# Local attention placed between the chunks of the projection that feeds it

## What is computed

```
z = h @ w_in
q, k, v = split_cols(z[..., :SWA_COLS], (SWA_Q_COLS, SWA_KV_COLS, SWA_KV_COLS))
o_a = swa_sink_attention(q, k, v, sinks, alibi_slopes(SWA_HEADS))
o_b = rwkv7_time_mix(z[..., SWA_COLS:], mu, w0, w2, a0, a2, g2, k_k, k_a, r_k, ln_g, ln_b)
o = jnp.concatenate([o_a, o_b], axis=-1).astype(h.dtype)
return o @ w_out
```

```
s = jnp.einsum('bnqgrd,bnkgd->bngrqk', qb, kb)
s = s - slopes * dist                    # -inf outside the window
m = jnp.maximum(jnp.max(s, axis=-1, keepdims=True), sink)
p = jnp.exp(s - m)
p = p / (jnp.sum(p, axis=-1, keepdims=True) + jnp.exp(sink - m))
o = jnp.einsum('bngrqk,bnkgd->bnqgrd', p, vb)
```

## Time and profile before

| | |
|---|---|
| time, median of 3 runs | 2430.26 us (2426.51 to 2432.41) |
| profiled execution, its own time | 2425.49 us |
| its span (first to last instruction) | 2423.7 us |
| PE busy | 2128.3 us, 88% |
| DVE busy | 1620.8 us, 67% |
| ACT busy | 992.0 us, 41% |
| mean granted TensorE clock | 0.91 |

### The profile page before, as it was taken

One profiled execution on the slowest core, in us unless ns is written; L12 is line 12 of the kernel. 1 busy time (PEld: TensorE's weight loads), 2 busy tenths in 40 slices (PEclk: granted clock), 3 DMA queues, 4 the chain that ended last, 5 costly groups with the idle time before them and its releaser, 6 DMA issues.

```text
span 2423.7 us, 35322 instructions
## 1 busy us (share of the span) xinstructions
PE 2128.3 (88%) x14424; PEld 1908.3 (79%) x14424; DVE 1620.8 (67%) x2579; ACT 992.0 (41%) x1572; POOL 0.2 (0%) x4
## 2 busy tenths in 40 slices
PE   7729679999888899999999878489999999768998
PEld 7619569999865699999999855369999999456998
DVE  4467479884155698878857879658787753276555
ACT  4321054454144554443345633244334332345332
POOL 0000000000000000000000000000000000000000
PEclk9769589999877899999989999789998998878999
DMA  7200038746220487667644310047766652303551
GB/s 295 93 0 1 1 136 298 279 140 226 94 98 1 152 286 275 234 234 276 254 148 158 139 53 1 0 165 262 282 225 245 237 183 90 132 1 108 199 188 70
DMA packets 114849, 379.33 MB, mean 157 GB/s; under 512 B 4993, under 2 KB 5121, under 8 KB 113921
## 3 DMA queue, kind: packets, MB, share of 16 engines
q1 hardware_dynamic: 114688, 377.08, 43.3%
HBM read 376.01 MB, written 1.05 MB: 156 GB/s over the span
## 4 chain that ended last, share of the span: by engine, by line
PE 72%; DVE 20%; ACT 4%; issue 3%; DMA 2%; DVEq 0%; SPq 0%; ACTq 0%
PE psum L873 29%; PE psum L889 14%; PE psum L651 7%; PE psum L704 4%; DVE htok L1854 2%; DVE buf L569 2%; PE psum L645 2%; PE psum L1130 2%; PE psum L1483 1%; PE psum L2272 1%; DMA ring<-in_w_ffn 1%; PE psum L1727 1%; PE psum L856 1%; DVE buf L2053 1%; PE psum L498 1%
## 5 line engine op out<-in xcount | busy, mean ns | idle before, releaser
L873 PEld LDWEIGHTS psum<-buf,buf 128*128 128x128 f32 x6048 | 741.5, 192 | 12.9 <-DVE buf L787 4.0
L873 PE MATMUL psum<-buf,buf 128*128 128x256 f32 x6048 | 746.2, 283 | 2.0 <-DVE buf L787 2.0
L889 PE MATMUL psum<-buf,buf 128*128 128x512 f32 x1584 | 384.1, 391 | 3.3 <-DVE buf L936 3.3
L889 PEld LDWEIGHTS psum<-buf,buf 128*128 128x128 f32 x1584 | 289.1, 188 | 59.7 <-DVE buf L936 5.0
L787 DVE TENSOR_TENSOR buf<-ring,buf 128x2048 fp32r<-128x2048 f32 x132 | 301.9, 2287 | 43.3 <-ACT buf L781 42.4
L651 PE MATMUL psum<-buf,buf 128*128 128x256 f32 x2064 | 255.0, 284 | 9.5 <-DVE buf L569 9.4
L651 PEld LDWEIGHTS psum<-buf,buf 128*128 128x128 f32 x2064 | 249.2, 192 | 15.0 <-DVE buf L569 15.0
L781 ACT ACTIVATE buf<-ring 128x2048 fp32r<-128x2048 f32 x132 | 251.3, 1904 | 20.3 <-DMA ring<-in_w_ffn 20.3
L803 DVE TENSOR_TENSOR buf<-ring,buf 128x1024 fp32r<-128x1024 f32 x132 | 161.5, 1223 | 144.4 <-ACT buf L798 144.1
L569 DVE TENSOR_TENSOR buf<-ring,buf 128x1024 fp32r<-128x1024 f32 x132 | 161.3, 1224 | 118.0 <-ACT buf L563 108.7
L798 ACT ACTIVATE buf<-ring 128x1024 fp32r<-128x1024 f32 x132 | 139.3, 1055 | 191.6 <-PE psum L889 189.1
(11 more groups left out here) (318 smaller groups left out, 2362.0 us busy)
## 6 DMA issues: line engine op xcount, KB each, us to landing
ring<-in_w_ffn SPq DMA_DIRECT2D x88, 1536.0 KB, 6.5
modw<-in_w_mod SPq DMA_DIRECT2D x98, 768.0 KB, 6.9
ring<-in_w_conv SPq DMA_DIRECT2D x44, 1536.0 KB, 6.5
ring<-in_w_ssd_in SPq DMA_DIRECT2D x16, 1536.0 KB, 6.6
ring<-in_w_ns_in SPq DMA_DIRECT2D x9, 1536.0 KB, 7.6
ring<-in_w_hy_in SPq DMA_DIRECT2D x7, 1536.0 KB, 19.2
ring<-in_w_ssd_out SPq DMA_DIRECT2D x5, 1536.0 KB, 6.5
ring<-in_w_cmp SPq DMA_DIRECT2D x4, 1024.0 KB, 4.7
```

The source lines that it names most:

```text
L873: ins = E.matmul(b[:, g * T:(g + 1) * T], w[:, wa, g, k, :], h[:, ha, k, :], start=k + n_ == 0, stop=k == KC - 1 and n_ == 2)
L889: ins = E.matmul(acc[:, t, g * 512:(g + 1) * 512], hr[z][:, ha, t * P:(t + 1) * P], wd[z][:, wa, g * 512:(g + 1) * 512], start=j == 0 and ...
```

## The change

The attention is no longer run after the projection but between its chunks:

- The columns of `w_in` are laid out with the values behind the keys, so the value chunk is chunk 6, and the recurrent chunks are 7 to 20.
- `main` takes the list of PSUM banks for its chunks (`ring_of`) and a function `tick(c)` that it calls at the end of each chunk's turn. The first stage gives banks 6 and 7; the other projections keep the default of 4 to 7.
- `attend` is divided: `attention` makes the five steps (with `back` divided into `normalize` and `turn`), and takes places for its buffers, the number of pairs of score banks (`nsc`) and the first banks of transposes and outputs. Here scores use banks 0-1 only, transposes 2-3, outputs 4-5. `attend` calls them in the order as before for the other two stages that use it.
- `tick` gives unit `n` its steps at fixed chunks: scores and exponentials at chunk `7 + 3n`, normalize at `8 + 3n`, turn at `9 + 3n`, outputs and their copy at `10 + 3n`. The outputs of unit `n` stand ahead of the scores of unit `n + 1` at the same chunk. The last step is at chunk 19.
- The scores wait only for ScalarE up to the evacuation of chunk 6.
- `Ring.used` of a slot is now a list to which every chunk of the load adds its point.

```diff
@@ -170,7 +170,7 @@
     row("k_head_g", i["mla_k_head_g_2"][0])
 
     hy = i["hy_w_in"][0]
-    hy = np.concatenate([hy[:, 0:512], twice(hy[:, 512:640], 2), hy[:, 768:2560], hy[:, 640:768]], 1)
+    hy = np.concatenate([hy[:, 0:512], twice(hy[:, 512:640], 2), hy[:, 640:2560]], 1)
     ns = i["nsa_w_in"][0]
     kc, vc, ks, vs, kw, vw = (ns[:, 1024 + 256 * j:1280 + 256 * j] for j in range(6))
     ns = np.concatenate([ns[:, 0:1024], twice(kc, 4), twice(vc, 4), twice(ks, 4), twice(kw, 4), vs, vw,
@@ -584,6 +584,7 @@
                 if c % 3 == 0:
                     m = min(3, n - c)
                     made["slot"], made["full"] = load(dram[name][c:c + m], m)
+                    Ring.used[made["slot"]] = []
                 s, full = made["slot"], made["full"]
                 raw = slot_ap(s, SLOT)[:, (c % 3) * CHUNK:(c % 3 + 1) * CHUNK]
                 if c in tokens:
@@ -591,7 +592,7 @@
                 else:
                     p = split_chunk(raw, wp[c % 3], full, wp_free[c % 3])
                     made[c] = (s, raw, p)
-                    Ring.used[s] = [p]
+                    Ring.used[s].append(p)
 
             def pre_a(free):
                 wp_free[0] = wp_free[1] = free
@@ -602,7 +603,8 @@
                 wp_free[2] = free
                 prepare(2)
 
-            def main(evac, h_pts):
+            def main(evac, h_pts, ring_of=(4, 5, 6, 7), tick=None):
+                nb = len(ring_of)
                 freed = [()] * 3 + [(Ring.sums_taken,)]
                 done = []
                 first = 0
@@ -618,16 +620,16 @@
                             for c in range(2):
                                 w = wp[c].rearrange("p a (k n) -> p a k n", k=KC)
                                 for n_, (wa, ha) in enumerate(PASSES):
-                                    ins = E.matmul(bank(4 + c)[:, 0:T], w[:, wa, k, :], h[:, ha, k, :], start=k + n_ == 0,
+                                    ins = E.matmul(bank(ring_of[c])[:, 0:T], w[:, wa, k, :], h[:, ha, k, :], start=k + n_ == 0,
                                                    stop=k == KC - 1 and n_ == 2)
                                 if k == KC - 1:
                                     done.append(pe.count(ins.then_inc(pe.sem, 1)))
                     wp_free[0:2] = [done[0]], [done[1]]
-                    freed[0] = evac(0, bank(4), done[0])
+                    freed[0] = evac(0, bank(ring_of[0]), done[0])
                 for c in range(first, n):
                     prepare(c + 1)
                     s, raw, point_w = made[c]
-                    b = bank(4 + c % 4)
+                    b = bank(ring_of[c % nb])
 
                     @block.tensor
                     def _(_e):
@@ -635,7 +637,7 @@
                         if c == 0:
                             for point in h_pts:
                                 E.wait_ge(*point)
-                        for point in freed[c % 4]:
+                        for point in freed[c % nb]:
                             E.wait_ge(*point)
                         if c in tokens:
                             w = raw.rearrange("p (k n) -> p k n", k=KC)
@@ -652,12 +654,14 @@
                                                    stop=k == KC - 1 and n_ == 2)
                         done.append(pe.count(ins.then_inc(pe.sem, 1)))
                     if c in tokens:
-                        Ring.used[s] = Ring.used[s][-1:] + [done[c]] if c % 3 else [done[c]]
+                        Ring.used[s].append(done[c])
                     else:
                         wp_free[c % 3] = [done[c]]
                     if c:
-                        freed[(c - 1) % 4] = evac(c - 1, bank(4 + (c - 1) % 4), done[c - 1])
-                evac(n - 1, bank(4 + (n - 1) % 4), done[n - 1])
+                        freed[(c - 1) % nb] = evac(c - 1, bank(ring_of[(c - 1) % nb]), done[c - 1])
+                    if tick is not None:
+                        tick(c)
+                evac(n - 1, bank(ring_of[(n - 1) % nb]), done[n - 1])
 
             return pre_a, pre_b, main
 
@@ -1003,13 +1007,15 @@
             return dict(pre_a=pre_a, pre_b=pre_b, run=run, gain=gain, shift=shift, h=h)
 
 
-        def attend(units, keys, ready, at):
+        def attention(units, keys, ready, at, pt_at=None, st_at=None, nsc=2, turn_bank=4, out_bank=6):
             ar = Region(at)
             s_buf = [ar.take(4 * keys).rearrange("p (h k) -> p h k", h=4) for _ in range(3)]
 
+            ar.at = ar.at if pt_at is None else pt_at
             pT = [[[ar.take(4 * P) for _ in range(u_blocks)] for u_blocks in
                    [max(u["blocks"] for u in units if u["branch"] == b) for b in sorted({u["branch"] for u in units})]]
                   for _ in range(2)]
+            ar.at = ar.at if st_at is None else st_at
             st = ar.take(3 * 16)
             state = {"s_free": [go] * 2, "p_free": [go] * 3, "t_free": go, "o_free": [go] * 2,
                      "pT_free": [go] * 2}
...
@@ -1074,8 +1080,7 @@
                         p = act.count(A.activation(xtra, xtra, ACT.Exp).then_inc(act.sem, 1))
                     u["exp"] = p
 
-            def back(n, u):
-                q = n % 2
+            def normalize(n, u):
                 nk = u["keys"]
                 s = s_buf[n % 3]
                 stats = st[:, 16 * (n % 3):16 * (n % 3) + 16]
@@ -1091,16 +1096,20 @@
                         vl(V.tensor_tensor(rs, rs, u["gates"], ALU.mult).then_inc(dve.sem, 1))
                     Ring.p = vl(V.tensor_tensor(s[:, :, 0:nk], s[:, :, 0:nk],
                                                 spread(rs.rearrange("p (h o) -> p h o", o=1), [P, 4, nk]), ALU.mult).then_inc(dve.sem, 1))
-                normed = Ring.p
+                u["normed"] = Ring.p
+
+            def turn(n, u):
+                nk = u["keys"]
+                s = s_buf[n % 3]
 
                 @block.tensor
                 def _(_e):
-                    E.wait_ge(*normed)
+                    E.wait_ge(*u["normed"])
                     E.wait_ge(*state["t_free"])
                     for b in range(u["blocks"]):
                         w = min(P, nk - b * P)
                         for i in range(4):
-                            ins = E.transpose(bank(4 + b)[0:w, i * P:(i + 1) * P], s[:, i, b * P:b * P + w], ident)
+                            ins = E.transpose(bank(turn_bank + b)[0:w, i * P:(i + 1) * P], s[:, i, b * P:b * P + w], ident)
                     Ring.p = pe.count(ins.then_inc(pe.sem, 1))
                 state["p_free"][n % 3] = Ring.p
 
...
@@ -1143,6 +1152,10 @@
 
 
 
+            return scores, exponentials, normalize, turn, outputs, outputs_copy
+
+        def attend(units, keys, ready, at):
+            scores, exponentials, normalize, turn, outputs, outputs_copy = attention(units, keys, ready, at)
             scores(0, units[0])
             for n in range(len(units) + 3):
                 if n + 1 < len(units):
@@ -1152,7 +1165,8 @@
                 if 2 <= n < len(units) + 2 and units[n - 2]["last"]:
                     outputs(units[n - 2])
                 if 1 <= n <= len(units):
-                    back(n - 1, units[n - 1])
+                    normalize(n - 1, units[n - 1])
+                    turn(n - 1, units[n - 1])
                 if n >= 3 and units[n - 3]["last"]:
                     outputs_copy(units[n - 3])
             return [(dve.sem, dve.n), (act.sem, act.n), (pe.sem, pe.n)]
@@ -1160,7 +1174,7 @@
 
         def hybrid():
             h = halves(H_AT, KC)
-            pre_a, pre_b, project = projection("w_hy_in", 21, h, tokens=(20,))
+            pre_a, pre_b, project = projection("w_hy_in", 21, h, tokens=(6,))
 
             def run(h_pts, nxt):
                 return hybrid_run(h_pts, project, nxt)
@@ -1200,13 +1214,13 @@
                     def _(_e):
                         A.wait_ge(*p)
                         Ring.q = act.count(A.activation(kT[:, c - 4, :], b[:, 0:T], ACT.Copy).then_inc(act.sem, 1))
-                elif c == 20:
+                elif c == 6:
                     @block.scalar
                     def _(_e):
                         A.wait_ge(*p)
                         Ring.q = act.count(A.activation(vtok, b[:, 0:T].rearrange("p (t d) -> p t d", t=NT), ACT.Copy).then_inc(act.sem, 1))
                 else:
-                    m = c - 6
+                    m = c - 7
                     dst = ([r_] * 4 + [k_] * 4 + [v_] * 4)[m][:, (m % 4) * T:(m % 4 + 1) * T] if m < 12 else \
                         (wa if m == 12 else glo)
 
@@ -1225,8 +1239,6 @@
                                                                  dst[:, 1:T], ALU.mult, ALU.add).then_inc(dve.sem, 1))
                 return (Ring.q,)
 
-            project(evac, h_pts)
-            projected = [(dve.sem, dve.n), (act.sem, act.n), (pe.sem, pe.n)]
             oT = hT
 
 
@@ -1244,7 +1256,27 @@
                              out=oT[:, 2 * g:2 * g + 2, t * P:(t + 1) * P])
                     u["parts"] = [u]
```

(28 more changed lines are left out.)

## The result

| | before | changed |
|---|---|---|
| median | 2425.84 us (7 runs, 2425.22 to 2432.41) | 2443.6 us (7 runs, 2437.21 to 2445.94) |
| profiled execution | 2425.49 | 2437.36 |
| tanh that begins the recurrent half | 108.30 | 120.34 |

A forecast was written before the change was run, and what follows sets the result against it. Projection bound by PE (TensorE). Work 9.6, pauses 19.0, chunk 2 0.4, tail 1.0, less 26.2 removed: +3.8; clock +8.9, low-rank -0.5: +12.2 us on 2430.3, said as 2442, range 2430 to 2450.

The forecast's parts named there:

- Pauses, 19.0 us: Projection loop: PE stands still before chunks 9, 12, 15, 18, as splits queue behind the softmax: 4.0, 5.5, 4.0, 5.5 us.
- Work on TensorE, 9.6 us: Projection loop: attention matmuls between chunks count in full on PE: scores 3.2, outputs 3.5, transposes 2.9 us.
- Clock, 8.9 us: Projection loop: half clock for 3.0 to 6.0 us after each of four pauses, costing 2.2 us each.
- Low-rank matmuls, -0.5 us: Behind the attention: these matmuls may begin at full clock; between 0 and -4.7 us, -0.5 taken.
- Chunk 2, 0.4 us: Projection start: with two banks chunk 2 waits for the evacuation of chunk 0, about 0.4 us once.
- Tail, 1.0 us: After chunk 20: its evacuation, the wait of the tanh (L1258) and hand-overs, 1.0 us.
- Sum: Whole kernel: all terms give +12.2 us, so 2437.7 us for an execution like the profiled one.
- The median, 2442: Whole kernel: +12.2 us added to the median of three timed runs, 2430.3, gives 2442.5, said as 2442.
- Rival A: Projection loop: splits keep ahead, no stall or clock drop, only PE's own work added: 2414.5 us; chance 0.13.
- B: Projection loop: the stalls come but the clock stays full: +3.8 us, 2434; chance 0.15.
- C: Projection loop: half clock holds longer, up to 4.7 us lost per pause: +22.6, 2453; chance 0.08.

The follow-up runs named there:

- the run with the steps spread alone: Changed kernel with only each unit's attention steps spread over more chunks, softmax divided by engine, two banks, split still behind the tick: 2413.22 us, ratio 0.993.
- The loop without pauses: Changed kernel with weight split ahead of the softmax, three projection banks and attention steps spread over more chunks: 2412.14 us, ratio 0.9944.
- the run with extra matmuls: Changed kernel with 24 or 36 unused matmuls put on TensorE where it stood idle behind the chunk after each unit's scores: 2429.35 us, ratio 1.0016.
- the run without them: Changed kernel with unused extra matmuls in TensorE's pauses, loop at full clock: chunk 2 to tanh 85.7 us, 7.0 less than 92.7; median 2429.35 us.
- the spread versions: Changed kernel with attention steps spread: alone 2413.22 us; with split ahead, ratio 0.9947; with split ahead and three banks, 2412.14 us.
- the run with split ahead and three banks: Changed kernel with the weight split ahead of tick(c) and projection banks 5 to 7, softmax still in the tick of its scores: ratio 1.0009.

## Why the prediction was right, step by step

- *Pauses, 19.0 us.* Measured 17.8: 3.70 and 5.19 where 4.0 and 5.5 stood. From the end of chunk 7 (45.84 in the chain of waits) to the restart at 53.25 it is 7.4 us where 7.6 stood, since neighbouring instructions of one engine overlap by 0.1 us in the rows; and PE finished chunk 8 3.7 us behind chunk 7 where 3.6 stood. The mechanism was the one predicted, down to the evacuation that the second bank adds; the run with the steps spread alone removed it by order, with the same instructions.
- *Work on TensorE, 9.6 us.* The chain of waits gives 0.67 and 1.09 for the scores (the prediction had 0.87 for the wide ones), 0.44 and 0.87 for the transposes (so they do halve with the clock), 0.59 and 1.07 for the outputs: 9.5 in total. The loop without pauses says 10.5. The 1 us more, which I had not counted, lies where TensorE changes from one kind of matmul to another: in the run with extra matmuls a chunk behind scores took 2.98 us from its first matmul to the next group's, and one behind transposes 3.04, where 2.88 is a chunk among chunks.
- *Clock, 8.9 us.* The chunks behind the pauses took 4.60, 4.46, 4.61 and 5.46 us on the chain where others took 2.87, and one unit's transposes 1.24 for 0.87: 8.0 us, and 7.0 by the run without them. Half clock lasted 3.4, 3.4, 3.4 and 6.8 us; counted from the restart on, as the prediction counts, it is 3.4, 3.0, 3.4 and 6.1 us, a mean of 4.0 in its range of 3.0 to 6.0, where it had taken 4.4. The Trainium skill (TensorE: Matmul & The Clock Gate, section "HAM oscillation — how this bites in real kernels") has, for the kernel that it describes, half of 1.67 us a pause, which would be 3.3 us in all; the trace has more than twice that, and the measurement decides.
- *Low-rank matmuls, -0.5 us.* Nothing: 9.3 us at 0.50 as in the earlier trace rows. That it could have been otherwise shows in the run with the steps spread alone, where they began at full clock (0.48 us for the first in place of 0.79).
- *Chunk 2, 0.4 us.* It waited 0.2.
- *Tail, 1.0 us.* The last chunk ended at 119.3 and the tanh began at 120.34: 1.0.
- *Sum.* Predicted 2437.7 for an execution like the profiled one, measured 2437.36. That it is this close is luck: 1.15 us of the difference is that chunk 2 began at 27.65 in place of 26.50; from there it is 10.9 us against 12.3 of my terms (all but chunk 2's and the low-rank matmuls'). Of the 1.15 us the wait for a bank is 0.2. The rest arose while chunks 0 and 1 were multiplied (7.15 us against 6.34). The profiled executions with two banks have chunk 2 at 26.31 to 27.81, the others at 25.79 to 26.52; whether the change has a part in it is not shown.
- *The median, 2442.* It was 2443.6, and this is luck too. I added 12.2 to a median that was 4.6 us high. What made up for it is the second group of executions, of which I had no notion: the prediction held that the stages after the first are unchanged, which is true of the profiled execution (no later stage moved by more than 1.8 us) and not of the median.

Rival A (splits keep ahead, 2414.5) is what the spread versions then did: 2412 to 2413. B fell with the first restart (the clock went to 0.50), and C with it (the clock was full again after 3.4 us, not 9.3).

## What to carry to other kernels

When independent work is put between the steps of a loop that TensorE bounds, sum the engines' busy time last and follow each queue first: a step that waits for a TensorE instruction of the same turn holds back everything written behind it, here the weights of the chunk after next. Give the long steps of the inserted work turns of their own, so that what they wait for is already done, and keep them from standing behind a step that must wait, such as the copy of outputs just written. With two banks the same instructions then cost 11.5 us in the loop (68.1 less 56.6) instead of 36.1 (92.7 less 56.6). Follow the inserted work's own instructions in TensorE's queue too. And before a few microseconds are believed, delay the kernel by one: if that alone moves it by twelve, only the stage's own interval can be compared.

## What the runs showed of the hardware that was not expected

- A pause of 1.98 us of TensorE in an otherwise dense loop was followed by a chunk of 4.59 us in place of 3.1 at a granted clock of 0.50, another like it in the same loop was not. The clock stayed full with pauses of 0.83 and 0.89 us (chunks of 3.10 us behind them) and with two of 1.72 us in the run with split ahead and three banks; in the loops it fell with each pause of 3.2 us or more. Ahead of the low-rank matmuls a pause of 3.2 us left it full once (run with the steps spread alone).
- The fall can come well behind the restart: 1.4 us of dense matmuls ran at full clock after a pause of 3.76 us before it fell.
- A copy of 1.0 us on ScalarE made the whole program 12.4 us longer in the median (2438.11 against 2425.71). In the profiled executions the loss lies where TensorE's clock differs, more than 70 us later and in the third stage.
